# Modulation products on four column strips of TensorE, summed by a product with ones; twelve of their slabs in the S5 stage; the projection's weights in three places

## The reference, cut to what matters

```
c_act = jax.nn.silu(c)                                  # (1, 1024)
mod = c_act @ w_ada[l] + b_ada[l]                       # (1, 6144): w_ada is 1024 x 6144, 24 MB
sh1, sc1, gt1, sh2, sc2, gt2 = jnp.split(mod, N_MOD, axis=-1)
a_in = modulate(rmsnorm(h, norm1_g[l]), sh1, sc1)       # h * (1 + scale) + shift
proj = a_in @ w_in[l]                                   # 256 x 1024 @ 1024 x 2568
u_s5, qkv, z, a_gate, b_gate = jnp.split(proj, splits, axis=-1)
y_s5  = s5_mixer(u_s5, ...)                             # a scan over 256 tokens, then a GLU
y_gdn = gdn_mixer(qkv, z, a_gate, b_gate, ...)          # chunks, each with a triangular inverse
mix = concatenate([y_s5, y_gdn]) @ w_out[l]
h = h + gt1[:, None, :] * mix
m_in = modulate(rmsnorm(h, norm2_g[l]), sh2, sc2)       # into the experts; gt2 scales their sum
```

## Time and profile before

| | |
|---|---|
| median of three runs | 2740.99 us (2738.6 to 2741.88) |
| profiled execution: its time, its span | 2738.65 us, 2736.9 us |
| PE busy / DVE / ACT / POOL | 2620.2 / 1729.5 / 1250.4 / 126.3 us |
| mean DMA rate over the span | 186 GB/s |
| start of the first projection matmul (L427) | 53.84 us |
| start of the first S5 group on PE (L1576) | 120.74 us |
| start of the delta rule's first product (L1724) | 186.97 us |

### The profile page before, as it was taken

How to read it: one execution, slowest core, us unless ns; L and a number is a source line. 1 busy time by engine, 2 the same in 40 slices (tenths; PEclk the granted TensorE clock), 3 DMA queues, 4 the chain that set the end, 5 groups by cost and what they waited for, 6 DMA issues and landing times.

```text
span 2736.9 us, 34632 instructions
## 1 busy us (share of the span) xinstructions
PE 2620.2 (96%) x14258; PEld 2216.3 (81%) x14258; DVE 1729.5 (63%) x1881; ACT 1250.4 (46%) x1587; POOL 126.3 (5%) x204
## 2 busy tenths in 40 slices
PE   7899799999899979999999999999899999998998
PEld 6788688878788868888888888888878888886887
DVE  5774487777556555665666666565665656646665
ACT  3420356666444454444445445444553444445443
POOL 4000000000000101000000001000010010000000
PEclk9999899999999999999999999999999999998999
DMA  8443268888365436556545655654446555554552
GB/s 258 149 153 105 78 245 296 300 285 308 126 214 186 161 116 222 192 176 218 193 155 200 206 191 172 209 191 138 140 139 215 185 200 185 169 168 132 201 185 92
DMA packets 331195, 509.85 MB, mean 186 GB/s; under 512 B 14896, under 2 KB 258640, under 8 KB 331040
## 3 DMA queue, kind: packets, MB, share of 16 engines
q1 hardware_dynamic: 324672, 484.70, 52.2%
q0 software_dynamic: 5792, 20.78, 2.3%
q10 hardware_dynamic: 576, 2.20, 0.2%
HBM read 506.56 MB, written 1.05 MB: 185 GB/s over the span
## 4 chain that ended last, share of the span: by engine, by line
PE 87%; DVE 7%; ACT 2%; DMA 1%; issue 1%; POOL 0%; SPq 0%; DVEq 0%; POOLq 0%; ACTq 0%
PE psum L427 19%; PE psum L428 18%; PE psum L429 18%; PE psum L816 15%; PE psum L817 8%; PE psum L1263 3%; DVE raw_r L414 1%; DVE wlo L414 1%; DMA raw<-in_w_ada 1%; PE psum L830 0%; PE psum L1724 0%; PE psum L584 0%; DVE small L2603 0%; PE psum L1805 0%; PE psum L1820 0%
## 5 line engine op out<-in xcount | busy, mean ns | idle before, releaser
L414 DVE TENSOR_TENSOR raw_r<-raw,whi 128x2048 fp32r<-128x2048 f32 x185 | 421.5, 2290 | 162.9 <-ACT whi L406 162.2
L406 ACT ACTIVATE whi<-raw 128x2048 fp32r<-128x2048 f32 x185 | 350.6, 1906 | 12.3 <-DMA raw<-in_w_up 9.7
L414 DVE TENSOR_TENSOR place_lo<-arena,place_hi 128x2048 fp32r<-128x2048 f32 x107 | 244.1, 2289 | 95.1 <-ACT place_hi L406 95.1
L817 PE MATMUL psum<-act_both,place_lo 128*128 128x256 f32 x944 | 264.1, 280 | 0.0
L904 ACT ACTIVATE scratch<-scratch 128x256 f32<-128x256 f32 x112 | 46.8, 418 | 462.7 <-DVE scratch L980 462.7
L816 PE MATMUL psum<-act_both,place_hi 128*128 128x512 f32 x704 | 247.9, 392 | 0.0
L816 PE MATMUL psum<-act_both,whi 128*128 128x512 f32 x640 | 228.4, 398 | 0.0
L406 ACT ACTIVATE place_hi<-arena 128x2048 fp32r<-128x2048 f32 x107 | 202.5, 1905 | 2.0 <-DMA arena<-in_ff_w_in 2.0
L817 PEld LDWEIGHTS psum<-act_both,place_lo 128*128 128x128 f32 x944 | 177.7, 188 | 2.4
L817 PE MATMUL psum<-act_both,raw_r 128*128 128x256 f32 x640 | 179.6, 281 | 0.0
L414 DVE TENSOR_TENSOR wlo<-wlo_f,wlo 128x2048 fp32r<-128x2048 f32 x61 | 139.6, 2289 | 58.8 <-ACT wlo L406 58.2
(11 more groups left out here) (555 smaller groups left out, 6149.1 us busy)
## 6 DMA issues: line engine op xcount, KB each, us to landing
arena<-in_ff_w_in SPq DMA_DIRECT2D x182, 512.0 KB, 4.9
raw<-in_ff_w_in SPq DMA_DIRECT2D x126, 512.0 KB, 4.7
arena<-in_ff_w_out SPq DMA_DIRECT2D x88, 512.0 KB, 4.5
raw<-in_ff_w_out SPq DMA_DIRECT2D x68, 512.0 KB, 4.6
wlo_f<-in_ff_w_in SPq DMA_DIRECT2D x44, 512.0 KB, 4.8
raw<-in_w_ada SPq DMA_DIRECT2D x20, 1024.0 KB, 5.4
raw<-in_w_gate SPq DMA_DIRECT2D x35, 512.0 KB, 4.4
raw<-in_w_up SPq DMA_DIRECT2D x35, 512.0 KB, 5.8
```

The costliest lines, as they stand in the source:

```text
L406: act.activation(hi, loaded, ACT.Copy).then_inc(S("slab_hi"), 1)
L414: dve.tensor_tensor(lo, loaded, hi.bitcast(F32), ALU.subtract).then_inc(S("slab_lo"), 1)
L817: last = pe.matmul(both[:, 0, :], lo[:, c, g, cs], act_hi[:, k, :], start=False, stop=k == KD - 1)
```

## The change: what it does

1. **Strips.** `ada_strips_pe` broadcasts each piece of `c_act` to 32 columns only, and runs four pieces side by side on the four column strips of the array, twice: eight matmuls of 32 x 256, whose four partial sums end on four groups of 32 partitions. ACT copies them to SBUF with a factor 1/32 (`ada_copy_act`), and a product with ones adds them up: `ada_rows_pe` (one matmul of 256 columns) for `gt1` and `gt2`, `ada_first_pe` (two matmuls of one column) for slabs 0 to 7, `ada_cols_pe` (32 matmuls of one column over four slabs) for `sh2` and `sc2`. DVE adds the bias to the finished sums; its products with the identity and its reductions go.
2. **Order of the slabs.** S5 multiplies slabs 8 to 19, the delta rule 20 to 23 ahead of the inverse, and the inverse holds none. In S5, DVE takes sums out between its adds and scans. The five small instructions on the gates (L1651 to L1655) stand ahead of the first S5 group.
3. **Opening.** The constants and `cols` are loaded in two pieces, a small one first. `x` is loaded ahead of slab 5. The S5 table steps of DVE stand ahead of all modulation work. The transposes stand ahead of slab 7 on PE. Groups of six small matmuls (`keep_clock`) follow slabs 3 to 6. ACT modulates 8 of the 16 tiles and DVE the other 8 (`pre_mod_dve`).
4. **Projection.** The slabs of `w_in` rotate over three weight buffers, and the loop on PE is written out. The loads of `s5_b`, the rest of `cols` and `mats` and of `b_ada` stand on SP between those of `w_in`.

```diff
-PLAN.add_order("w_in", (0, 1) * 5)
+PLAN.add_order("w_in", (0, 1, 2) * 3 + (0,))
...
-            for k in range(KD):
-                last = pe.matmul(ada_bank(j), c_act[:, k:k + 1].to_broadcast([P, P]), slab[:, k, :], start=k == 0, stop=k == KD - 1)
-            last.then_inc(S("ada_used"), 1)
+            for kk in range(2):
+                for q in range(4):
+                    k = 2 * q + kk
+                    last = pe.matmul(psum[32 * q:32 * q + 32, ada_bank(j), 0:256], c_act[:, k:k + 1].to_broadcast([P, 32]), slab[:, k, :],
+                                     start=kk == 0, stop=kk == 1)
+            last.then_inc(S("ada_used"), 1)
+
+        def ada_copy_act(act, j):
+            act.wait_ge(S("ada_used"), j + 1)
+            act.activation(ada_part(j), psum[:, ada_bank(j), 0:256], ACT.Copy, scale=1 / 32)\
+               .then_inc(S("proj_evac" if j < ADA_FIRST else "ada_copied"), 1)
+
+        def ada_first_pe(pe, j):
+
+            pe.wait_ge(S("proj_evac"), j + 1)
+            for k in range(2):
+                at = 256 + 2 * (j // 2) + k
+                last = pe.matmul(psum[:, ada_bank(j), at:at + 1], ada_part(j)[:, k * P:(k + 1) * P], mat("ones")[:, 0:1], start=True, stop=True)
+            last.then_inc(S("ada_summed"), 1)
+
+        def ada_rows_pe(pe, j):
+
+            pe.wait_ge(S("ada_copied"), j - ADA_FIRST + 1)
+            pe.matmul(psum[:, ada_bank(j), 256:512], mat("ones"), ada_part(j), start=True, stop=True).then_inc(S("ada_summed"), 1)
+
+        def ada_cols_pe(pe, j):
+
+            pe.wait_ge(S("ada_copied"), j + 3 - ADA_FIRST + 1)
             for k in range(KD):
...
+                for c in range(4):
+                    picked = ada_part(j + c).rearrange("p (i k) -> p k i", k=KD)[:, k, :]
+                    last = pe.matmul(psum[32 * c:32 * c + 32, 7, 256 + k:257 + k], picked, mat("ones")[:, 0:1], start=True, stop=True)
+            last.then_inc(S("ada_summed"), 1)
+
+        def ada_rows_dve(dve, j):
+
+            dve.wait_ge(S("ada_summed"), ADA_SUMMED[j])
+            dve.wait_ge(S("bias_loaded"), 32)
+            row = mod[:, j * 256:(j + 1) * 256]
+            dve.tensor_tensor(row, row, psum[:, ada_bank(j), 256:512], ALU.add).then_inc(S("ada_evac"), 1)
...
+        def pre_mod_dve(dve):
+
+            dve.wait_ge(S("mod_cols"), 1)
+            for q, (t, k0, nk, bank) in enumerate(PIECES[2:]):
+                dve.wait_ge(S("transposed"), q + 3)
+                for c in range(nk):
+                    k = k0 + c
+                    last = dve.tensor_scalar(act_f[:, k, t * P:(t + 1) * P], psum[:, bank, c * P:(c + 1) * P],
+                                             modc[:, 1, k:k + 1], modc[:, 0, k:k + 1], ALU.mult, ALU.add)
+                last.then_inc(S("act_f"), nk // 2)
...
-                if lv in INV_ADA:
-                    ada_pe(pe, INV_ADA[lv])
...
+            for j in range(ADA_FIRST):
+                if j == 5:
+                    pre_act(act, 0)
+                ada_copy_act(act, j)
             head_act(act, "w_in", 0)
...
+            pre_mod_act(act)
+            head_act(act, "w_in", 1, 2)
...
-            for j in range(ADA_FIRST):
-                ada_pe(pe, j)
+            ada_strips_pe(pe, 0)
             pe.wait_ge(S("mats_loaded"), 16)
+            for j in range(1, ADA_FIRST - 1):
+                ada_strips_pe(pe, j)
+                ada_first_pe(pe, j - 1)
+                if j >= 3:
+                    keep_clock(pe, 0, 6)
+            ada_first_pe(pe, ADA_FIRST - 2)
             pre_pe(pe, 0)
+            ada_strips_pe(pe, ADA_FIRST - 1)
+            ada_first_pe(pe, ADA_FIRST - 1)
```

More of the change, by code:

```diff
@@ L64 @@
                ("c_re", S5_TILES * 32), ("c_im", S5_TILES * 32)])
-MATS = {name: i for i, name in enumerate(["ident", "upto", "ones", "flip"] + [f"level{k}" for k in range(LEVELS)])}
+FIRST_COLS = COLS["c_re"][0]
+FIRST_MATS = 2
+MATS = {name: i for i, name in enumerate(["ident", "ones", "upto", "flip"] + [f"level{k}" for k in range(LEVELS)])}
 def constants():
     i, j = np.arange(P)[:, None], np.arange(P)[None, :]
-    mats = [i == j, i <= j, np.ones((P, P), bool), i + j == P - 1]
+    mats = [i == j, np.ones((P, P), bool), i <= j, i + j == P - 1]
     for k in range(LEVELS):
@@ L1290, in mod_dve @@
-        def mod_dve(dve, done, shift, norm):
-            for q in (shift, shift + 1):
-                done(dve.tensor_tensor(modc[:, q, :], modc[:, q, :], col("b_ada", q * KD, KD), ALU.add))
+            for kk in range(2):
+                for q in range(4):
+                    k = 2 * q + kk
+                    last = pe.matmul(psum[32 * q:32 * q + 32, ada_bank(j), 0:256], c_act[:, k:k + 1].to_broadcast([P, 32]), slab[:, k, :],
+                                     start=kk == 0, stop=kk == 1)
@@ L1461, in w_in_pe @@
         def w_in_pe(pe):
-            cols_pe(pe, "w_in", 0, 10, ADA_FIRST, 0)
+            gates_pe(pe, 0)
+            for j in range(10):
+                if j == 1:
+                    gates_pe(pe, 1)
+                elif j == 8:
+                    s5_pairs_pe(pe)
+                s, n = slab_at("w_in", j)
+                pe.wait_ge(lo_ready[s], n + 1)
+                pe.wait_ge(S("proj_evac"), ADA_FIRST + j - 1)
+                proj_t(pe, slab_views(s, KD), 4 + j % 2, act0=None if j else 0).then_inc(slab_used[s], 1)
         lb_rows = [act_f[:, 4 + 2 * i:6 + 2 * i, :].rearrange("p k t -> p (k t)").rearrange("p (m s) -> p m s", m=CS5) for i in range(2)]
@@ L1518, in w_in_dve @@
             for j in range(10):
-                next_lo(dve, "w_in", j, 10)
-                if j < 3:
-                    (s5_bl_dve, s5_c_dve, s5_cl_dve)[j](dve, done)
+                if j == 0:
+                    s5_c_dve(dve, done)
+                elif j == 1:
+                    s5_cl_dve(dve, done)
                 if 2 <= j < 8:
@@ L1583, in s5_pe, with out @@
             pe.wait_ge(S("s5_act"), S5_ACT["s5_pairs"][5])
[L1584 to L1590 removed]
+            def out(m):
                 if m >= 2:
@@ L1603, in s5_pe @@
                 last.then_inc(S("s5_y"), 1)
+            pe.wait_ge(S("mats_loaded"), 32)
+            bu(0)
+            ada_strips_pe(pe, 8)
+            pe.wait_ge(S("s5_dve"), S5_DVE["gate_in"][0])
+            ada_strips_pe(pe, 9)
+            bu(1)
+            ada_rows_pe(pe, 8)
+            ada_rows_pe(pe, 9)
+            out(0)
+            ada_strips_pe(pe, 10)
+            ada_strips_pe(pe, 11)
+            bu(2)
+            ada_rows_pe(pe, 10)
+            ada_rows_pe(pe, 11)
+            ada_strips_pe(pe, 12)
+            ada_strips_pe(pe, 13)
+            out(1)
+            ada_strips_pe(pe, 14)
+            ada_strips_pe(pe, 15)
+            bu(3)
+            ada_cols_pe(pe, 12)
+            ada_strips_pe(pe, 16)
+            ada_strips_pe(pe, 17)
+            out(2)
+            ada_strips_pe(pe, 18)
+            ada_strips_pe(pe, 19)
+            ada_cols_pe(pe, 16)
+            out(3)
             pe.wait_ge(S("qk_sq"), 2)
@@ L1642, in s5_dve @@
                 dve.tensor_tensor(p2, p2, ei, ALU.mult).then_inc(S("s5_states"), 1)
-                for i in ADA_OF_GROUP[m]:
-                    ada_dve(dve, done, ADA_FIRST + i)
                 if m:
@@ L2773, in _ @@
             cols_load(sp, "w_in", w_in, 0, 1)
+            sp.wait_ge(S("ada_used"), ADA_FIRST)
+            cols_load(sp, "w_in", w_in, 2)
             sp.wait_ge(S("s5_pool"), S5_POOL["table"][6])
             sp.dma_start(arena[:, 14336:15360], a["s5_bt"]).then_inc(S("s5_b_loaded"), 16)
-            cols_load(sp, "w_in", w_in, *range(2, 10))
-            sp.wait_ge(S("ada_used"), ADA_FIRST)
+            sp.wait_ge(S("pre_sums"), 2 * NT)
+            sp.dma_start(junk, a["s5_b"]).then_inc(S("s5_b_loaded"), 16)
+            sp.dma_start(cols[:, FIRST_COLS:], a["cols"][:, FIRST_COLS:]).then_inc(S("cols_loaded"), 16)
+            cols_load(sp, "w_in", w_in, 3)
+            sp.dma_start(mats[:, FIRST_MATS:, :].rearrange("p m n -> p (m n)"), a["mats"][:, FIRST_MATS * P:]).then_inc(S("mats_loaded"), 16)
+            cols_load(sp, "w_in", w_in, 4)
+            for part in (2, 5):
+                gate = slice(part * D, (part + 1) * D)
+                sp.dma_start(mod[:, gate], a["b_ada"][:, gate].to_broadcast([P, D])).then_inc(S("bias_loaded"), 16)
+            cols_load(sp, "w_in", w_in, *range(5, 10))
             load(sp, GD, PLAN.base["w_glu"][GD], a["w_glu"].rearrange("(k p) n -> p k n", p=P))
@@ L2928, in _ @@
             head_dve(dve, "w_in", 1)
+            s5_bl_dve(dve, done)
+            head_dve(dve, "w_in", 2)
             w_in_dve(dve, done)
```

243 lines of the change are left out of this document (120 added, 123 removed).

## The result

The changed kernel takes 2759.99 us (median of five runs, 2753.97 to 2762.56) against 2741.12 us for the kernel before on the same chip. The ratio is 1.0061, with a 95% interval of 1.0047 to 1.0075: slower by 0.6%, where 2712.5 us had been forecast. The profiled execution took 2759.99 us, with a span of 2757.8 us.

What follows compares the result with a forecast made beforehand. PE was taken as the bound (87% of the chain), DVE in S5; -6.9 - 3.2 + 0.8 - 4.0 - 13.7 = -27.0 against 2738.65 gave 2711.6, stated as a median of 2712.5 us, range 2703 to 2722.

Steps and rivals of the forecast that it cites:

- The inverse: Delta rule's inverse: levels 1 to 4 lose their slab, 8.97 to 5.56 us each, and the last pick goes; -13.7 us.
- Rival D: Inverse at half clock without slabs: levels 1 to 6 take 11.1 us each, +19.7 there, 2745 in all; chance 0.02.
- S5: S5 groups: slab 8's DMA wait goes, but DVE waits for sums in mid-group; +0.8 us with four more slabs done.
- rival A: S5 grows by more: PE falls to half clock between short bursts; 7 us in all, 2719; chance 0.17.
- The head sums and the GLU: Stretch behind S5, the 16 columns of L1708 and the GLU: claimed unchanged, 0 us.
- The opening: Start to the gates: cheap strip slabs and an earlier root on POOL bring the gates from 50.41 to 43.5; -6.9 us.
- rival E: Strips don't overlap: 3.7 us a slab plus sums, S5 some +12, 2728 in all; chance 0.03.
- The one price without a row: The 32 one-column matmuls on strips: taken as 0.9 us, between 0.2 and 7.4.
- The projection: Gates to S5 input: with three weight buffers, PE's one wait on DVE for slab 5 goes; -3.2 us.
- Ahead of the inverse: Delta rule before the inverse: four slabs on strips, DVE no longer waits for slabs or picks; -4.0 us.
- The rest: Everything behind the inverse: the same code, shifted by one constant; 0 us.
- The last line of the sum: Terms sum to 2711.6; the median lies 2.3 above the profiled execution, so 2712.5 was given.

Runs made afterwards that it cites:

- second and third experiment: Second: changed kernel plus 8 long matmuls ahead of the inverse, 2733.61 us. Third: kernel before, its four inverse slabs moved ahead of the inverse, 2745.56 us.
- the last experiment: Changed kernel with root first on GpSimd, S5 sums late, 4 long matmuls ahead of the inverse and 5 ahead of the `kb` wait: 2706.97 us.
- the run with full-width slabs: Changed kernel with slabs 20 to 23, ahead of the inverse, at full width instead of on strips: 2769.86 us.
- the 4 long: Changed kernel plus 4 matmuls of 256 columns in TensorE's wait ahead of the inverse: five executions at 2729 to 2731 us, five at 2754 to 2770.
- the 8 short: Changed kernel plus 8 matmuls of 64 columns in TensorE's wait ahead of the inverse: six executions at 2728 to 2733 us, four at 2755 to 2766.
- the sums late: Changed kernel with S5's modulation sums at each group's end, slabs 12, 13 and 17 behind outputs: 2749.85 us.

## Why the prediction was wrong

**The inverse, forecast -13.7, came to +13.9: this step failed, and with it the forecast.** It said that levels 1 to 4 lose their slab and go from 8.97 to 5.56 us. They lost it, and all six levels went to 10.24. Rival D had named this, priced at 11.1 us a level and 2745 in all, and was given 0.02. The argument against it was true and missed the point: levels 5 and 6 held the full clock without a slab, and so do all levels when they are entered at full clock (second and third experiment). What I did not ask is how they are entered. Before, TensorE came into the inverse out of 3.6 us of slab 19, with no wait ahead of its first product and one of 0.82 us behind it (slab 19; the second product):

```profile
210.01 3.62 PE L1263 MATMUL psum<-raw,small 128*128 128x256 f32 x16
...
215.33 1.25 PE L1822 MATMUL psum<-mats,arena 128*128 128x128 f32 x8 [0.82 <-DVE arena L1926]
```

In my own sum the part ahead of the inverse got 4 us shorter because TensorE had less to do than VectorE; that is the same as saying that TensorE would wait for VectorE there. I took the gain and did not price the wait. Removing work that had covered a handover of 1.74 us cost 28 us.

In a sentence apart: the Trainium skill ("TensorE: Matmul & The Clock Gate", HAM oscillation) says that idle gaps between bursts put the engine back to half rate, by an example with longer gaps than here; at the entry of the inverse the trace shows the fall behind gaps of 1.74 and 0.35 us, and the prediction cited it for S5 alone. The same page of the Trainium skill (What's actually happening) says that the monitor's window runs freely and isn't reset at the kernel's start, so that the point of a change varies; this would fit the two kinds of execution, which no run here ties to a window.

**S5, forecast +0.8, came to +7.2.** Counted from the projection's end, the groups were to start at 5.9, 17.3, 31.7 and 43.3 us and the last skip to end at 56.7; the trace has 5.8, 17.1, 31.6, 44.4 and 63.1. So groups 0 and 1 came out as priced (the wait in group 1 is 4.87 for 4.7), and the steps that failed are in groups 2 and 3. The first is the wait for the column sums, 3.73 and 4.69 us for 2.5 and 1.7: I had left out that the four slabs of a column sum stood in the same queue. The second is the clock of the last outputs, which the sum took as full. Those of groups 2 and 3 ran at half, 4.3 us from 157.40 and 4.4 from 171.15, where each took 2.4 before:

```profile
157.40 1.93 PE L1627 MATMUL psum<-arena,cols 128*32 128x128 f32 x32 [0.95 <-DVE arena L1711]
159.26 0.80 PE L1624 MATMUL psum<-arena,act_f 128*128 128x128 f32 x2
159.99 1.94 PE L1627 MATMUL psum<-arena,h_f 128*32 128x128 f32 x32
```

By these rows half clock is an estimated 3.9 of the 6.4 us that were missing, partly inside the wait of 4.69; rival A, which named the clock and 7 us, was right in part. Moving the sums gave 9.8 us at much the same clock, so the order was enough to win the stage: a sum that the scans don't need stood ahead of them, behind an output that waits for the group before. No run here tests the clock alone.

**The head sums and the GLU, forecast as unchanged, came to +3.7**: mostly L1789 at half clock, 6.99 us in place of 3.80, behind 5.23 us of idle time in S5. Missed altogether. In the last experiment it is 3.73.

**The opening, -5.1 for -6.9.** The root was to start at 31.9 and started at 35.53. My sum had VectorE's step out of GpSimd's way; it put the two at the same time, and they slowed each other (2.96 for 1.90). That is 3.0 of the 3.6 us: GpSimd's last two table steps took 9.1 and 4.6 us for 7.0 and 3.7. The steps behind the root came out quicker than in my sum. The strips were right (1.07 us at full clock, 1.94 at half), and so rival E is out. The one price without a row, the 32 one-column matmuls on strips, came to 1.2 us for 0.9 (L1286).

**The projection, -2.5 for -3.2**: right; no wait of L434 for VectorE is left. It ran at half clock for its first 4.8 us where it did for 2.7 before, by an estimate 0.9 us of loss.

**Ahead of the inverse, -1.1 for -4.0**: the 16 products of L1864 ran in part at half clock, 5.44 for 3.81 us, behind an idle time of 2.76: the same cause, one stage earlier, and 1.6 of the 2.9 us. VectorE also waited 3.65 us for L1852, with TensorE busy up to it; the sum had no such wait.

**The rest, +4.8 for 0**: +1.8 in the chunk steps, which begin at half clock (L1913 2.08 us, 1.16 before), and +3.0 behind. I have no cause for the latter; from that norm's root to another some 730 us later, traces with the same code differ by up to 4 us (728.8 for the kernel before, 732.8 for its variant with the slabs ahead); the changed kernel has 731.7, so the +3.0 lies in that stretch.

**The last line of the sum** has a slip: 2711.6 and 2.3 make 2713.9, not 2712.5. It is small beside the rest.

What stays open is why the same program keeps its clock in one execution and loses it in the next.

## What to carry to other kernels

When a change takes work off TensorE, look at every wait that this work had covered, and at what follows it: price that stretch at half clock, and give it far more than the 0.02 given here, since a long run of short matmuls kept whichever clock it began with. A few matmuls on constants ahead of the wait are cheap cover, and should last clearly longer than the wait. A result that is not needed yet should be taken out of an in-order queue's way: at the end of the group, not where it happens to be ready.

## What the runs showed of the hardware

- TensorE stayed at 1.2 GHz for 61 us while busy 5.00 of every 5.00 us with matmuls of 64 columns, and held 2.4 GHz through the 37 us of the same inverse when it entered at 2.4. Other matmuls brought it back soon: some 2 us after the start of a burst of 256 columns, and within 5 us in the chunk steps of 128 columns behind the inverse (half clock from 281.45, full at 285.92), although these held waits of 0.84 and 0.69 us.
- It fell behind an idle time of 1.74 and one of 0.35 us, with the 20 us ahead at 1.00 (the run with full-width slabs); in other executions it survived the same two. A single wait of 0.84 us at the end of an inverse at full clock lowered it in four traces of nine.
- Three edits (the 4 long, the 8 short, the sums late) gave two separate groups of times, 22 to 28 us apart at their nearest, not a spread: in such a case the single executions tell more than the median.
- VectorE and GpSimd slow each other on large elementwise work: 1.22 to 2.92 us for a 128x1024 product on VectorE, 1.90 to 2.96 on GpSimd, 1.87 to 5.13 for four scalings of 128x512.
